# Scan level 3: where the turned forward keys stand on TensorE

## What is computed

```python
def step(s, inp):
    r_t, w_t, k_t, v_t, kk_t, a_t = inp
    sa = jnp.einsum('bhij,bhj->bhi', s, -kk_t)
    s = (s * w_t[:, :, None, :] + sa[..., None] * (kk_t * a_t)[:, :, None, :]
         + v_t[..., None] * k_t[:, :, None, :])
    return s, jnp.einsum('bhij,bhj->bhi', s, r_t)
```

## Time and profile before

| | us |
|---|---|
| median of 3 runs | 2904.25 (2904.25 to 2905.07) |
| profiled execution | 2902.43 |
| its span in the trace | 2900.5 |
| PE busy | 2828.7 (98%) |
| DVE busy | 1864.6 (64%) |
| ACT busy | 1356.4 (47%) |
| POOL busy | 251.0 (9%) |
| mean granted clock of TensorE | 0.996 of full speed |

### The profile page before, as it was taken

How to read it: one execution, slowest core, us unless ns; L and a number is a source line. 1 busy time by engine, 2 the same in 40 slices (tenths; PEclk the granted TensorE clock), 3 DMA queues, 4 the chain that set the end, 5 groups by cost and what they waited for, 6 DMA issues and landing times.

```text
span 2900.5 us, 56865 instructions
## 1 busy us (share of the span) xinstructions
PE 2828.7 (98%) x24171; PEld 2393.2 (83%) x24171; DVE 1864.6 (64%) x2553; ACT 1356.4 (47%) x1963; POOL 251.0 (9%) x303
## 2 busy tenths in 40 slices
PE   6999999999999999999999999999999999999998
PEld 2687888888888878888888888888888888888887
DVE  3597876777777776664445556799875555554444
ACT  3222446566665444444444444566544444444443
POOL 1000002333422000000000000133100000000000
PEclk8999999999999999999999999999999999999999
DMA  9997880000000668875665656666556666666564
GB/s 386 366 380 253 283 268 29 8 8 13 8 8 20 214 201 260 261 247 184 189 191 176 202 190 209 190 183 180 174 183 192 187 192 186 191 189 202 186 193 160
DMA packets 470782, 532.31 MB, mean 184 GB/s; under 512 B 22920, under 2 KB 422722, under 8 KB 469634
## 3 DMA queue, kind: packets, MB, share of 16 engines
q1 hardware_dynamic: 464754, 516.13, 55.4%
q0 software_dynamic: 3408, 10.42, 1.1%
q10 hardware_dynamic: 2368, 2.11, 0.3%
HBM read 522.29 MB, written 4.19 MB: 182 GB/s over the span
## 4 chain that ended last, share of the span: by engine, by line
PE 91%; DVE 4%; DMA 2%; ACT 1%; issue 1%; SPq 0%; DVEq 0%; ACTq 0%
PE ps L2468 14%; PE ps L2479 14%; PE ps L2481 14%; PE ps L2480 14%; PE ps L2644 11%; PE ps L2469 7%; PE ps L2971 4%; PE ps L2972 2%; PE ps L2490 2%; PE ps L2492 2%; PE ps L2491 2%; DMA raw<-in_w_mod 1%; PE ps L2654 1%; PE ps L2652 1%; PE ps L2540 1%
## 5 line engine op out<-in xcount | busy, mean ns | idle before, releaser
L1580 DVE TENSOR_TENSOR lo<-raw,hi 128x1024 fp32r<-128x1024 f32 x776 | 948.4, 1228 | 708.7 <-ACT hi L1063 703.7
L1063 ACT ACTIVATE hi<-raw 128x1024 fp32r<-128x1024 f32 x776 | 820.1, 1059 | 1067.8 <-PE ps L2481 602.0
L2479 PE MATMUL ps<-hi,mov 128*128 128x512 f32 x1408 | 553.2, 393 | 3.6 <-DVE mov L1648 3.6
L2481 PE MATMUL ps<-hi,mov 128*128 128x512 f32 x1408 | 549.0, 390 | 0.0
L2480 PE MATMUL ps<-lo,mov 128*128 128x512 f32 x1408 | 548.6, 390 | 0.0
L2479 PEld LDWEIGHTS ps<-hi,mov 128*128 128x128 f32 x1408 | 264.8, 188 | 58.4 <-issue 4.4
L2481 PEld LDWEIGHTS ps<-hi,mov 128*128 128x128 f32 x1408 | 264.6, 188 | 55.8
L2480 PEld LDWEIGHTS ps<-lo,mov 128*128 128x128 f32 x1408 | 264.9, 188 | 53.8
L2468 PE MATMUL ps<-mov,hi 128*128 128x512 f32 x864 | 305.7, 398 | 0.4 <-DVE mov L2398 0.3
L2468 PE MATMUL ps<-hid,hi 128*128 128x512 f32 x704 | 244.3, 394 | 0.0
L2469 PE MATMUL ps<-mov,lo 128*128 128x256 f32 x864 | 242.3, 280 | 0.0
(11 more groups left out here) (439 smaller groups left out, 4279.7 us busy)
## 6 DMA issues: line engine op xcount, KB each, us to landing
raw<-in_w_in SPq DMA_DIRECT2D x184, 512.0 KB, 4.8
raw<-in_w_gate SPq DMA_DIRECT2D x176, 256.0 KB, 2.9
raw<-in_w_up SPq DMA_DIRECT2D x176, 256.0 KB, 3.2
raw<-in_w_down SPq DMA_DIRECT2D x88, 512.0 KB, 3.4
raw<-in_w_ffn_gate SPq DMA_DIRECT2D x176, 256.0 KB, 2.9
raw<-in_w_ffn_up SPq DMA_DIRECT2D x176, 256.0 KB, 3.1
raw<-in_w_ffn_down SPq DMA_DIRECT2D x88, 512.0 KB, 4.5
raw<-in_w_out SPq DMA_DIRECT2D x64, 512.0 KB, 4.5
```

The lines of the kernel that those rows point to most:

```text
L1063: act.activation(hi[:, s, :, :], src, ACT.Copy).then_inc(hi_ready, 1)
L1580: dve.tensor_tensor(lo[:, s, :, :], raw_at(ph, i, j)[0], hi[:, s, :, :].bitcast(F32), ALU.subtract)\
L2479: pe.matmul(out, x(k)[:, 0, tokens], w_hi, start=first, stop=False)
L2481: mm = pe.matmul(out, x(k)[:, 1, tokens], w_hi, start=False, stop=last)
```

## The change

In level 3 the call between the two groups of products gets an empty range, and the call behind the second group gets all four chunks. The wait for `oMV`, which goes with chunk 0, goes with it. In the other levels both ranges are what they were.

```diff
                         each(scan_pe[d], d, (q, f"Y{l}"), 2, lambda c, hs: LEV[l][d][hs, c, :], lambda c, hs: XT[q][d][hs, c, :])
-                    between(b, q, l, ahead, range(0, 1))
+                    between(b, q, l, ahead, range(0, l != 3))
                     for d in range(2):
                         scan_act[d].wait(pe, (q, f"Yb{l}"), b)
                         scan_dve[d].wait(pe, (q, f"X{l - 1}"), b)
                         each(scan_pe[d], d, (q, f"T{l}"), 0, lambda c, hs: XY[d][hs, c, 0, :], lambda c, hs: XY[d][hs, c, 1, :])
-                    between(b, q, l, ahead, range(1, NC))
+                    between(b, q, l, ahead, range(l != 3, NC))
                     behind_level(b, q, l, ahead, norm)
```

## The result

| | before | after |
|---|---|---|
| median of 4 runs, us | 2904.25 (2903.04 to 2905.07) | 2889.00 (2887.25 to 2889.24) |
| profiled execution, us | 2902.43 | 2889.24 |
| its span, us | 2900.5 | 2887.3 |
| mean granted clock | 0.996 | 0.995 |

The ratio is 0.9946, 95% interval 0.9931 to 0.9960: the kernel is 15.25 us (0.53%) faster, against 12.0 us forecast. The direction and the price of the removed wait held. The profiled executions differ by less, 13.2 us. What follows asks what else is in the difference.

What follows compares the result with a forecast made beforehand. TensorE, busy 98% of the span, was taken to bound the kernel; removing 0.75 us of idle in each of 16 scan units gives 12.0 us, so 2904.25 - 12.0 = 2892.25 us, range 2890.0 to 2897.5 us.

Steps and rivals of the forecast that it cites:

- What bounds, and the cause: Scan, level 3: TensorE sets the pace; T3 queues behind key products waiting for oMV, 12.0 us in 16 waits.
- (a) T3 early: Level 3, Y3 to T3: falls from 2.03 to 1.16 us with nothing between, gaining 0.87 us.
- the lower bound: A bubble of 0.05 to 0.1 us between Y3 and T3 would leave 0.69 us per unit, 11.0 us.
- (b) The moved records: Level 3, T3 to Y4: four key records add 0.12 us, 1.28 becomes 1.40; the oMV wait is filled, cover 0.28.
- (c) The sum: Level 3, Y3 to Y4: 3.31 becomes 2.56 us, 0.75 less per unit, 12.0 us over 16 units.
- Does the gain survive: Stations after T3: work on DVE, ACT and POOL that does not move still leaves room, so 12.0 us stays.
- ACT's and DVE's rooms: Free time left in level 3: ACT 0.24 us before Yb4, DVE 0.30 us before its subtraction of T3.
- rivals 1 and 2: Rival 1: late ACT work returns part of the gain, 2897.0 us, chance 0.08; rival 2: wait replaced, about 2903 us, chance 0.04.
- Later levels and the next unit are released by TensorE's own results and move along: Scan after level 3: later levels and next units move ahead with TensorE; no further term in the sum.
- rival 3: Scan, TensorE's instruction supply: removing idle brings more unexplained gaps, 0.6 us each; 30 more give 2910.3 us; chance 0.02.
- the four gaps listed for TensorE's products: Scan: four gaps of up to 0.6 us which no engine explains, 2.1 us in all.
- The low end of the range: Whole kernel: range starts at 2890.0 us, just below 2890.35, where the 0.87 us per unit counts in full, 13.9 us.

Runs made afterwards that it cites:

- e2: The changed order of products, with a wait for oMV put back ahead of T3; 2898.57 us, ratio 0.9988 to the kernel before.
- e13: e2 run again unaltered: products moved, wait for oMV kept ahead of T3; 2900.66 us, ratio 0.9990 to the kernel before.
- e11: The changed kernel, with ACT also copying oMV of direction 0 early, ahead of Yb2; 2890.51 us, ratio 0.9957 to the kernel before.
- e12: The kernel before, run again unaltered for a second trace; 2903.86 us, ratio 1.0002 to the kernel before.
- e9: The changed kernel, run again unaltered on another occasion; 2891.15 us, ratio 0.9956 to the kernel before.
- e3: The kernel before with 32 more full-array products at the start, whose results nobody reads; 2902.53 us, ratio 0.9999 to the kernel before.
- e5: The kernel before with 64 extra products of 64x64x64 at the start, behind the first transpose; 2902.75 us, ratio 1.0002 to the kernel before.

## Why the prediction missed by three microseconds

**What bounds, and the cause: right.** TensorE stood 16 times for 0.75 us at key products which T3 did not need. e2 and e13 show it from the other side: with the wait back ahead of T3, the 12.0 us of waits are back.

**(a) T3 early: right.** 1.14 us for 1.16; the bubble ahead of T3 was 0.02 us, where the lower bound had 0.05 to 0.1. **(b) The moved records: right**, 1.44 us for 1.40; the wait for oMV behind T3 was filled, and e11 shows that filling it earlier gives nothing. **(c) The sum: right as the price of the wait.** Yb3 to Yb4 gave 12.2 us in the first pair of traces and 11.9 in the mean of five.

**Does the gain survive: right.** ACT's and DVE's rooms came out within 0.03 us, rivals 1 and 2 did not occur, and the stages behind the scan kept their pace (299.84 of 300 us busy).

**The step that failed** is the one that says the rest of the scan stays as it was: "Later levels and the next unit are released by TensorE's own results and move along", and with it rival 3, which took the gaps without releaser as something that could only grow. The sum had this term at nothing. The kernel before held 0.4 to 4.7 us of them between Yb4 and Yb5, and moving the products alone took them away: four traces with the products moved and the wait kept have none, five of before have 2.5 in the mean. With the wait removed as well there are some again, 1.0 in the mean. So the term measured 1.5 us of gain in the mean, and 4.4 in the first pair of traces. I had counted 2.1 us for the whole scan from the four gaps listed for TensorE's products. The shorter stretched groups, such as T4 of the fifth unit, were not in that list; the unit-by-unit distances from Yb4 to Yb5 would have shown 4.7.

**The low end of the range** was the second error. It had 2.3 us below the forecast, from the bounds of the wait alone. Neither the gaps nor the spread of the measurement were in it: the kernel before has runs from 2898.8 to 2907.8 us on the later occasions (e12 with them), and its median moved between 2901.97 and 2904.25. On the second occasion (e9) the changed kernel took 2891.15 us and the gain was 12.1 us. The 95% interval of the first comparison, 0.9931 to 0.9960, still holds the forecast ratio of 0.9959: that the first median fell outside the range is in part chance. The mean gain of the five pairs, 13.0 us, would have given 2891.2 us, inside the range. Of the 15.25 us, about 12 are the wait, 1 to 2 the gaps on average; what remains, about 2 us, is how gaps, the way into the scan and the stages behind it fell in these executions. This last part is inferred from the spread, not shown run by run; the profiled pair, 13.2 us apart, does not have it.

**What stays open** is why the gaps come. They lie inside groups of products with nothing to wait for, several at the same place in two traces, which speaks for the supply of instructions. In the kernel before, sixth unit, the traffic of the DMA engines around the gap is nothing but two bursts, 33 GB/s for 0.5 us, that is 16.5 KB each (stretch, length, TensorE busy, clock, share, GB/s):

```profile
618.50:620.30 1.80, 1.80 (x67) 1.00 0.00 0
620.30:620.80 0.50, 0.50 (x19) 1.00 0.12 33
620.80:624.00 3.20, 2.67 (x78) 1.00 0.00 0
624.00:624.50 0.50, 0.50 (x26) 1.00 0.11 33
```

That is the size of a packet of the instruction queue. The first burst is 4.0 us behind Yb3 (616.53), the next 3.7 later, with the gap in between. In e13 the bursts of the same unit are 2.2 us behind Yb3 and then 4.9 us apart, and there is no gap. All sixteen traces agree on the tie. Between 455 and 935 us they have 42 places where two neighbouring TensorE records of one group of `each` start 0.25 us or more apart, 11 of them in the first trace of before. Each of the 42 ends 2.2 to 2.9 us behind the start of a packet of the instruction queue, although these packets come only every 4.5 to 5.1 us (the median of each trace). The 22 shorter ones, from 0.15 us, end 2.2 to 3.8 us behind one. The four traces with the wait kept have none of either sort, with as many packets (94 from 455 to 920 us, before 93, changed 96). So a block that comes late fits; no run changed the supply itself, so it is not shown as the cause. Why the moved products keep the gaps away, and why a block is late only at times, was not found. The Trainium skill, "Runtime: NRT & Kernel Launch", section "Instruction fetch mechanics", has the crossing from one block to the next mostly hidden. The traces agree with it for most packets: 93 in the first trace of before, 11 with such a gap behind them.

## What to carry to other kernels

When filler work waits for something that the work behind it does not need, put the filler where its wait is already filled; the price of the wait can be read to a few hundredths of a microsecond by comparing with a level that has no filler. Look at the order in which the releasing engine does its copies: the filler here waited for the third of four. When a gain below one per cent is at stake, take the same distance in every unit of the trace, not only the listed waits, and repeat the comparison before an excess is given a cause.

## What the runs showed of the hardware

- A product of 64x64x64 in alternating halves of the array costs 29 ns a record in the scan, while the ballast of e3, 128x128 weights with 64 columns, cost 217 ns a record (13.91 us for 64). I had not expected a factor of seven. Part of it is the place and not the shape: the ballast of e5, of the scan's own shape, took 6.19 us for 128 records at the start. Its records come 53 ns apart at first and 29 ns apart from about 14.4 us on, and the profile puts the granted clock at 1.00 (2.4 GHz) in both stretches, as in all of e3's ballast. Why the first ones are slower is not shown. The group, and two stretches of 1 us (length, busy us of each engine, clock, DMA share, GB/s):

```profile
9.45 6.19 PE L2532 MATMUL ps<-basics 64*64 64x64 f32 x128
```

```profile
12.50:13.50 1.00, 1.00 (x24) 1.00 (x24) 0.00 (x0) 1.00 (x2) 0.00 (x0) 1.00 1.08 433
14.50:15.50 1.00, 1.00 (x40) 1.00 (x36) 0.00 (x0) 0.00 (x0) 0.00 (x0) 1.00 1.04 391
```

- DVE's scan instruction of 128x260 takes from 687 to 1282 ns in one trace of before (the line gives least, median and greatest). From the third unit on, the first one of a context unit's pair has one of two durations in all sixteen traces, 0.69 or 1.27 to 1.29 us. In two context units of the first trace the same pair took 2.36 and 1.76 us:

```profile
L1902 DVE TENSOR_TENSOR_SCAN dirs<-kscan,dirs x32: 687/1060/1282, 443.3 to 882.3; 128x260 f32<-128x260 f32 x32
```

```profile
519.99 2.36 DVE L1902 TENSOR_TENSOR_SCAN dirs<-kscan,dirs 128x260 f32<-128x260 f32 x2
...
580.39 1.76 DVE L1902 TENSOR_TENSOR_SCAN dirs<-kscan,dirs 128x260 f32<-128x260 f32 x2
```

  TensorE's Y2 waits for what stands behind it, and the distance from Yb1 to Yb2 is 3.2 instead of 2.6 us in those units: 2 to 7 units of a trace, in the same kernel 3 once and 4 another time. The long ones cost 0.6 us each, so this alone moves an execution by up to 3 us.
